# Routed experts on one core: tokens packed behind each other, gathered once, and taken by ScalarE at an address read from memory

## The chip, the cores and the metric

The kernel runs on one core of a Trainium2 chip. The metric is the device time of one execution in microseconds (us). TensorE is PE in the profile, VectorE is DVE, ScalarE is ACT, GpSimd is POOL; SyncE (SP) issues most transfers.

## The reference

Two transformer blocks over 256 tokens of width 1024, all in float32. The first mixes tokens (stick-breaking attention, an mLSTM and a spatial gate), then sends each token to 2 of 32 experts; the second has a short convolution, an attention and two convolutional feed-forward layers. Only the experts of the first block are touched here:

```python
g_top = argmax(xt @ rg_w + rg_b)                  # one of 4 groups
e_val, e_loc = top_k(e_in, 2)                     # two of its 8 experts
e_w = softmax(e_val) * g_w
hb = silu(xb @ w_gate[e]) * (xb @ w_up[e])        # xb: the tokens of expert e, 1024 -> 256
y  = y.at[row_tok].add((hb @ w_down[e]) * wt)     # 256 -> 1024, added to each token's row
```

Each expert has 3 MB of weights, 96 MB for all 32; a token goes to two of them, so an expert has 16 tokens on average.

## The kernel before, in words

**Weights.** All weights come as one stream of units of 128x2048 floats (1 MB) in the order of use. SP fetches unit n into one of four raw buffers as soon as DVE has done with unit n-4. A matmul in float32r rounds its operands, so each unit is split: ACT writes the high part (`split`, a copy with rounding, L529, or in halves at L538), DVE the low part (raw minus high, L1194, halves at L1205). High and low parts have three buffers each, freed when PE has used the unit (`unit_used`). An expert has two units for gate and up and one for down; two experts make a pair, with its six units 0 to 5: expert 0's gate-up in 0 and 1, expert 1's in 2 and 3, and the two down units in 4 and 5. There are 16 pairs. The first two and the last two are written out, the twelve between them are three rounds of a loop of four pairs on PE, ACT and DVE.

**Tokens.** The router (DVE, small operations on 128x64 and less) marks the two chosen experts of each token in `sel`. Three small matmuls (`ranked`) count the tokens of each expert ahead of each token; that count is the token's slot, and each expert has 64 slots. For a group of four experts (a quad, two pairs) `pick_quad` compares the slot numbers with 1 to 64 (L1559), which gives a 0/1 matrix of tokens by 4x64 slots. `gather` (L2431) multiplies the tokens, high part and low part, with it, one block of 128 channels at a time, into one bank of 512 columns: 256 slots of the high part and 256 of the low part. ACT (`gather_out`, L749) or DVE copies that to `xg`. A quad's eight blocks are gathered during the two pairs before it, four in each pair; so all pairs but the last two gather. Tokens above 64 for one expert go another way, behind a branch on `spill_count`; the branch is not taken with these inputs.

**A pair.** `pair_gate_up` multiplies the 64 slots, high and low as 128 columns of the array, with the high and the low part of a unit: 16 matmuls of 512 columns an expert (L2448, L2449). The result has the slots' high part in rows 0 to 63 and the low part in rows 64 to 127. ACT copies it out (`gate_up_out`, L754), PE turns its four blocks (`turn_rows`, four transposes, L2456), and DVE adds the two halves (`fold`, L1608). ACT takes SiLU of the gate half (`silu_pair`, L758), DVE multiplies with the up half (`hidden`, L1613), ACT rounds the product (`hidden_high`, L762) and DVE makes its low part (`hidden_low`, L1617). `pair_down` makes the down product, 12 matmuls an expert (L2042 to L2044). `turn_slots` turns the pick matrix, ACT copies it (`back_out`, L766), DVE sums the slots' weights (`slot_weights`). In the next pair ACT and DVE scale and split the result (`y_high`, L773, and `y_low`, L1626) and PE adds it to the tokens' rows (`scatter`, L2500, L2501).

**The order.** Every engine has its order written out by hand. In `pair_act` it is: second half of unit 0; unit 1; `y_high`; units 2 and 3; `gate_up_out` 0; unit 4; two gather evictions; SiLU 0; unit 5; `gate_up_out` 1; `hidden_high` 0; eviction; `back_out`; eviction; SiLU 1; first half of the next pair's unit 0; `hidden_high` 1. In the last two pairs unit 5 is split ahead of SiLU 0. PE does gate-up 0, scatter, two gathers, turn 0, gate-up 1, a gather, `turn_slots`, turn 1, a gather, down 0, down 1; in the last two pairs turn 0 stands between the two units of gate-up 1.

Of the kernel before, what the change touches and what calls it, by code (L numbers as in the profile page):

```python
# [119 lines left out]
ARENA = A_QKA + 8 * T  # L120
A_FINAL = 3072
# [8 lines left out]
def program(nc, stream, table, params, finals, p_in, x_in, out):  # L130
    ctx = ExitStack()
    with ctx:
# [15 lines left out]
        xres = sb("xres", [P, TT, D])  # L148
        xn = sb("xn", [P, TT, D])
# [18 lines left out]
        spill_count = sb("spill_count", [1, 1], mybir.dt.int32)  # L168
        cwn = sb("cwn", [P, 2, 12])
# [33 lines left out]
        for name, width in [("gt", 16), ("lf", 8), ("la", 8), ("ccol", 16), ("den", 8), ("ssb", 8), ("msb", 8),  # L203
# [4 lines left out]
                            ("sel", 64), ("key", 64), ("over", 64), ("spill", 1), ("wslot", 1)]:  # L208
# [54 lines left out]
        xg = [a.rearrange("p (k e w s) -> p k e w s", k=KD, e=4, w=2)  # L263
              for a in (arena_r[:, 6144:10240], xs[:].rearrange("p w k t -> p (w k t)"))]

        gu = arena[:, 0:1024].rearrange("p (e n) -> p e n", e=2)
        gut = arena[:, 1024:1536].rearrange("p (e f s) -> p e f s", e=2, f=4)
# [179 lines left out]
        def overflow_pe(pe):  # L447
            with pe.If(spilled(pe) > 0):
# [10 lines left out]
                pe.wait_ge(S("over_ready"), 1)  # L459
# [34 lines left out]
        def _(sp):  # L494
# [5 lines left out]
            sp.dma_start(cst[:, P:], table[:, P:]).then_inc(S("table_loaded"), 16)  # L500
# [15 lines left out]
        def _(act):  # L516
# [194 lines left out]
            act.dma_start(g2_row, finals[2]).then_inc(S("final_loaded"), 16)  # L711
            act.dma_start(p_t, p_in).then_inc(S("p_loaded"), 16)
# [33 lines left out]
            def gather_out(buf, k, n, at):  # L746

                act.wait_ge(S("gathered"), n)
                act.activation(xg[buf][:, k].transpose([0, 2, 1, 3]), bank[at][:].rearrange("p (w e s) -> p w e s", w=2, e=4),  # L749
                               ACT.Copy).then_inc(S("gather_out"), 1)  # L750

# [4 lines left out]
            def silu_pair(x, e):  # L756
                act.wait_ge(S("summed"), x.count(2, e + 1))
                act.activation(sgl[:, e], gut[:, e, 0:2, :], ACT.Silu).then_inc(S("pair_silu"), 1)  # L758
# [17 lines left out]
            def pair_act(x):  # L776
# [3 lines left out]
                def out(m):  # L780
                    if not x.last_quad:
                        gather_out(1 - x.buf, 4 * x.second + m, x.count(4, 9 + m), 2 + m % 2)
# [35 lines left out]
            pairs(act, pair_act)  # L818
# [256 lines left out]
        def _(pool):  # L1075
# [26 lines left out]
            ins.then_inc(S("router_scaled"), 1)  # L1102
# [81 lines left out]
        def _(dve):  # L1184
# [365 lines left out]
            dve.tensor_tensor(dv, v2, v1, ALU.subtract).then_inc(S("router_diff"), 1)  # L1550
            dve.wait_ge(S("ranked"), 1)
            dve.scalar_tensor_tensor(two(V("key")), bank[0][:, 128:192].rearrange("p (a e) -> p a e", a=TT), 1.0,
                                     sel.bitcast(F32), ALU.add, ALU.mult).then_inc(S("routed"), 1)
# [14 lines left out]
            def gather_out(k, n, at):  # L1568

                dve.wait_ge(S("gathered"), k + 1)  # L1570
                dve.tensor_copy(xg[0][:, k].transpose([0, 2, 1, 3]),
                                bank[at][:].rearrange("p (w e s) -> p w e s", w=2, e=4)).then_inc(S("gather_dve"), 1)

            dve.wait_ge(S("routed"), 2)
            pick_quad(slice(0, 4), 0, S("pick_ready"))
            token_rest(1)
            link(dve.tensor_scalar(V("over"), V("key"), float(SLOTS + 1), None, ALU.is_ge))
# [24 lines left out]
            pick_quad(slice(4, 8), 1, S("pick_ready"))  # L1602
            split_to(U_MOE + 3)

            def fold(x, e):

                dve.wait_ge(S("rows_turned"), x.count(2, e + 1))
                dve.tensor_reduce(gut[:, e], bank[e][:].rearrange("p (f w s) -> p f s w", f=4, w=2), AX.X, ALU.add)\  # L1608
                   .then_inc(S("summed"), 1)

            def hidden(x, e):
                dve.wait_ge(S("pair_silu"), x.count(2, e + 1))
                dve.tensor_tensor(hv[:, e], sgl[:, e], gut[:, e, 2:4, :], ALU.mult).then_inc(S("hidden_ready"), 1)  # L1613
# [23 lines left out]
            def pair_dve(x):  # L1637
# [10 lines left out]
                if not x.second and x.p0 and not x.last_quad:  # L1648
# [4 lines left out]
                    quad_weights(four, 1 - x.buf, S("pick_ready"))  # L1653
                ahead(2)
                ahead(3)

                if x.last_quad:
                    split_part(x.unit(4), 0)
                    fold(x, 0)
                    split_part(x.unit(4), 1)  # L1660
                    hidden(x, 0)
                    hidden_low(x, 0)
                    fold(x, 1)
                    slot_weights(x)
                    hidden(x, 1)
                    split_part(x.unit(5), 0)
                    hidden_low(x, 1)
                    split_part(x.unit(5), 1)
                    return
                fold(x, 0)  # L1670
                ahead(4)
                hidden(x, 0)
# [361 lines left out]
        def _(pe):  # L2034
# [470 lines left out]
            def pair_step(x):  # L2505
# [27 lines left out]
                if x.p0:  # L2533
                    pe.wait_ge(S("summed"), x.count(2))
# [425 lines left out]
```

## Time and profile before

| | |
|---|---|
| median of 3 runs | 1088.3 us (1086.83 to 1090.26) |
| the profiled execution | 1087.57 us, its span 1085.6 us |
| busy in the span | PE 1058.6, DVE 866.3, ACT 714.3, POOL 144.1 |
| mean granted TensorE clock | 0.996 of 2.4 GHz |
| moved from HBM | 230.85 MB |
| expert stage | from the first gate-up matmul at 156.42 us to the end of the last down product at 449.49 us, 293.1 us |

The span reaches from the first to the last instruction; what lies around it is 2.0 us. A matmul's end in the profile is modelled, so matmuls that follow each other overlap in it: the distance from start to start is what one costs. ACT's and DVE's instructions overlap a little too, by some 0.1 us.

### The profile page before, as it was taken

The numbers are of one execution on the slowest core, as the hardware profiler recorded it, in microseconds if no ns is written. First come the engines' busy times: TensorE is split into PE (matmuls) and PEld (weight loads), VectorE is DVE, ScalarE is ACT, GpSimd is POOL, SyncE is SP. The second block draws the span as 40 slices with busy tenths as digits, with TensorE's granted clock in tenths as the row PEclk, the third lists the DMA queues.
The fourth block names the chain that finished last, engine by engine and source line by source line (L and its number), as shares of the span: only waits on it lengthen the run. The fifth ranks groups of instructions, "written<-read, shape, count | busy, mean of one in ns | idle before, by whom it ended". The sixth has DMA issues, their size and how long they took to land.

```text
span 1085.6 us, 17366 instructions
## 1 busy us (share of the span) xinstructions
PE 1058.6 (98%) x6390; PEld 925.0 (85%) x6390; DVE 866.3 (80%) x1142; ACT 714.3 (66%) x962; POOL 144.1 (13%) x96
## 2 busy tenths in 40 slices
PE   7999989999999999999999999999999999999997
PEld 6877778888788887789989899998788889999986
DVE  5498689999999999877666777677777877876876
ACT  6676479898889898775435545445566766455553
POOL 3001100000000000012000334250200000432420
PEclk9999999999999999999999999999999999999999
DMA  9541528889988888754654454554433335545531
GB/s 369 189 155 39 206 82 347 348 346 333 346 331 337 343 344 334 285 209 156 225 180 178 155 213 161 206 193 155 173 137 118 116 120 211 207 156 217 184 126 40
DMA packets 33605, 232.64 MB, mean 214 GB/s; under 512 B 3856, under 2 KB 3984, under 8 KB 6032
## 3 DMA queue, kind: packets, MB, share of 16 engines
q1 hardware_dynamic: 32688, 229.98, 57.3%
q10 hardware_dynamic: 864, 1.93, 0.6%
q8 instruction: 35, 0.57, 0.2%
q14 instruction: 18, 0.15, 0.0%
HBM read 230.85 MB, written 1.05 MB: 214 GB/s over the span
## 4 chain that ended last, share of the span: by engine, by line
PE 78%; DVE 12%; ACT 5%; DMA 2%; issue 2%; POOL 0%; SPq 0%; DVEq 0%; ACTq 0%
PE bank L2042 11%; PE bank L2044 11%; PE bank L2043 11%; PE bank L2600 9%; PE bank L2601 8%; PE bank L2602 8%; DVE wlo L1194 4%; PE bank L2449 4%; PE bank L2448 4%; PE bank L2431 2%; ACT whi L529 2%; DMA raw<-stream 2%; DVE arena L1797 2%; PE bank L2456 1%; DVE wlo L1205 1%
## 5 line engine op out<-in xcount | busy, mean ns | idle before, releaser
L1194 DVE TENSOR_TENSOR wlo<-raw,whi 128x2048 fp32r<-128x2048 f32 x178 | 405.7, 2288 | 62.9 <-ACT whi L529 62.3
L529 ACT ACTIVATE whi<-raw 128x2048 fp32r<-128x2048 f32 x197 | 375.0, 1913 | 76.3 <-PE bank L2044 37.6
L2600 PE MATMUL bank<-xs,whi 128*128 128x256 f32 x896 | 251.2, 280 | 1.5 <-DVE wlo L1194 1.5
L2601 PE MATMUL bank<-xs,whi 128*128 128x256 f32 x896 | 250.2, 279 | 0.0
L2602 PE MATMUL bank<-xs,wlo 128*128 128x256 f32 x896 | 250.0, 279 | 0.0
L2600 PEld LDWEIGHTS bank<-xs,whi 128*128 128x128 f32 x896 | 168.4, 188 | 3.8 <-DVE wlo L1194 2.3
L2601 PEld LDWEIGHTS bank<-xs,whi 128*128 128x128 f32 x896 | 168.4, 188 | 0.9
L2602 PEld LDWEIGHTS bank<-xs,wlo 128*128 128x128 f32 x896 | 168.4, 188 | 0.0
L2042 PE MATMUL bank<-whi,rounded 128*128 128x512 f32 x344 | 138.4, 402 | 1.1 <-DVE wlo L1194 0.4
L2044 PE MATMUL bank<-whi,rounded 128*128 128x512 f32 x344 | 136.1, 396 | 0.0
L2043 PE MATMUL bank<-wlo,rounded 128*128 128x512 f32 x344 | 136.0, 395 | 0.0
L2042 PE MATMUL bank<-whi,xs 128*128 128x512 f32 (+1 forms) x304 | 121.0, 398 | 2.8 <-DVE xs L1312 0.9
L1155 POOL COPY cwn<-par 128x12 f32 (+1 forms) x22 | 93.3, 4247 | 199.5 <-DVE arena L1797 199.4
L2044 PE MATMUL bank<-whi,xs 128*128 128x512 f32 (+1 forms) x304 | 118.3, 389 | 0.0
L2043 PE MATMUL bank<-wlo,xs 128*128 128x512 f32 (+1 forms) x304 | 118.2, 389 | 0.0
L1797 DVE SCALAR_TENSOR_TENSOR arena<-arena,cwn 128x255 f32<-128x255 f32 (+1 forms) x160 | 66.7, 480 | 34.6 <-ACT arena L846 33.9
L846 ACT ACTIVATE arena<-arena,cwn 128x256 f32<-128x256 f32 x80 | 34.2, 499 | 86.2 <-DVE arena L1786 86.2
L1087 POOL TENSOR_SCALAR total<-sumsq 128x1 f32<-128x1 f32 x14 | 7.2, 512 | 628.7 <-ACT xn L563 628.2
L1205 DVE TENSOR_TENSOR wlo<-raw,whi 128x1024 fp32r<-128x1024 f32 x66 | 79.2, 1220 | 1.9 <-ACT whi L529 1.7
L2042 PEld LDWEIGHTS bank<-whi,rounded 128*128 128x128 f32 x344 | 64.6, 188 | 18.1 <-issue 3.6
L2044 PEld LDWEIGHTS bank<-whi,rounded 128*128 128x128 f32 x344 | 64.6, 188 | 15.6
L2043 PEld LDWEIGHTS bank<-wlo,rounded 128*128 128x128 f32 x344 | 64.7, 188 | 13.1
(342 smaller groups left out, 1655.2 us busy)
## 6 DMA issues: line engine op xcount, KB each, us to landing
raw<-stream SPq DMA_DIRECT2D x215, 1024.0 KB, 4.9
arena<-finals ACTq DMA_DIRECT2D x3, 512.0 KB, 5.6
xres<-x_in SPq DMA_DIRECT2D x2, 512.0 KB, 4.8
raw<-stream SPq DMA_DIRECT2D x4, 256.0 KB, 6.1
out<-xn SPq DMA_DIRECT2D x4, 256.0 KB, 2.1
par<-params SPq DMA_DIRECT2D x1, 844.0 KB, 12.4
cst<-table SPq DMA_DIRECT2D x1, 502.0 KB, 8.8
arena<-p_in ACTq DMA_DIRECT2D x1, 256.0 KB, 5.9
```

The source lines that it names most:

```text
L529: act.activation(whi[:, s, :], raw[:, a, :], ACT.Copy).then_inc(S("high_done"), 1)
L1155: pool.tensor_copy(cwn[:, b, :], src).then_inc(S("taps_ready"), 1)
L1194: dve.tensor_tensor(wlo[:, s, :], raw[:, unit0 % RAW, :], whi[:, s, :].bitcast(F32), ALU.subtract)\
L1205: ins = dve.tensor_tensor(wlo[:, s, w], raw[:, unit0 % RAW, w], whi[:, s, w].bitcast(F32), ALU.subtract)
L1797: ins = dve.scalar_tensor_tensor(a, fraw[:, b, f, 0:T - 2 + k], cwn[:, b, 4 * k + f:4 * k + f + 1], a, ALU.mult, ALU.add)
L2042: pe.matmul(o, ah, bh, start=start, stop=False, skip_group_check=True)
L2043: pe.matmul(o, ah, bl, start=False, stop=False, skip_group_check=True)
L2044: return pe.matmul(o, al, bh, start=False, stop=stop, skip_group_check=True)
L2448: pe.matmul(bank[e][:], tokens, whi[:, s, c], start=kk == 0, stop=False, skip_group_check=True)
L2600: pe.matmul(o, whi[:, s, w], xhi[:, kk, :], start=first, stop=False, skip_group_check=True)
L2601: pe.matmul(o, whi[:, s, w], xlo[:, kk, :], start=False, stop=False, skip_group_check=True)
L2602: ins = pe.matmul(o, wlo[:, s, w], xhi[:, kk, :], start=False, stop=kk == 7, skip_group_check=True)
```

## The change

**Places instead of slots.** All tokens of all experts are packed behind each other, expert after expert, in 512 places. DVE sums `sel`, makes a running sum over the experts (`tensor_tensor_scan`) and from it where each expert begins; two wider matmuls give each token's place (`place`) and each expert's first place (`offs`, held at most 64 below the end of what is gathered, `first_place` as integers). For a token, its two places are the largest and the rest of the sum over the experts.

**One gather.** `pick_places` makes tokens by 256 places: a mask of one place and, with it added, of the other. Half 0 (places 1 to 256) is gathered ahead of pair 0, half 1 during pairs 0 and 1, four gathers in each. Pairs 2 to 13 gather nothing. The gathered tokens lie with high and low part of one place beside each other.

**Windows.** `take(p, e)` reads the expert's first place into a register of ACT and copies the 64 places from there to `window[e]`, in two instructions of 128x512. It is done for the pair to come: expert 0's behind SiLU 1, expert 1's at the pair's end. ACT's pairs are now all written out; PE and DVE keep their loop.

**Halves summed in the turn.** `turn_rows` is four float32 matmuls with `stack`, 128x64, with a one where row // 2 equals the column: it turns and adds high and low part at once. `fold` is gone; SiLU and `hidden` read the bank.

**Order.** Turn 0 stands between the two units of gate-up 1 in every pair, SiLU 0 ahead of unit 5 in every pair, and DVE does units 4 and 5 in halves around `hidden` and `hidden_low` in every pair. The pick of a quad's slots (`pick_quad`) stays for the scatter.

```diff
-            ins.then_inc(S("routed"), 1)
+            link(ins)
+            sel_f, tot, upto_ = sel.bitcast(F32), V("tot"), V("upto_")
+            link(dve.tensor_tensor(tot, sel_f[:, 0], sel_f[:, 1], ALU.add))
+            link(dve.tensor_tensor_scan(upto_, tot, tot, 0.0, ALU.add, ALU.max))
+            dve.tensor_tensor(places[:, 0:3:2], same(upto_, NE), same(tot, NE), ALU.subtract)
+            dve.tensor_tensor(places[:, 1], upto_, sel_f[:, 1], ALU.subtract).then_inc(S("routed"), 1)
...
+            link(dve.tensor_tensor(offs, bank[0][:, 192:224], last_place, ALU.min))
+            dve.tensor_copy(first_place[:], offs[0:1, :]).then_inc(S("routed"), 1)
+            link(dve.scalar_tensor_tensor(place, bank[0][:, 128:192].rearrange("p (a e) -> p a e", a=TT), 1.0,
+                                          sel_f, ALU.add, ALU.mult))
+            dve.tensor_reduce(V("pmax"), place, AX.X, ALU.max)
+            link(dve.tensor_reduce(V("psum"), place, AX.X, ALU.add))
+            link(dve.tensor_tensor(V("pmin"), V("psum"), V("pmax"), ALU.subtract))
+
+            def pick_places(half):
+                w = slice(T * half, T * half + T)
+                for t in range(TT):
+                    ins = dve.tensor_scalar(mask[:, t], iota[:, w], V("pmax")[:, t:t + 1], None, ALU.is_equal)
+                link(ins)
+                for t in range(TT):
+                    ins = dve.scalar_tensor_tensor(gpick[half][:, t], iota[:, w], V("pmin")[:, t:t + 1], mask[:, t],
+                                                   ALU.is_equal, ALU.add)
+                ins.then_inc(S("gpick_ready"), 1)
...
+            def take(p, e):
+
+                if p == PAIRS:
+                    return
+                if p:
+                    act.wait_ge(S("unit_used"), U_MOE + 6 * (p - 1) + 2 * e + 2)
+                act.wait_ge(S("gather_out"), 6 if p < 2 else 14)
+                place = act.value_load(first_place[0:1, 2 * p + e:2 * p + e + 1], min_val=0, max_val=2 * T - SLOTS)
+                for i in range(2):
+                    act.activation(window[e][:, 4 * i:4 * i + 4, :],
+                                   xg[i].rearrange("p k s w -> p k (s w)")[:, :, bass.ds(place * 2, 2 * SLOTS)], ACT.Copy)                       .then_inc(S("window_ready"), 1)
...
-                if x.last_quad:
-
-                    ahead(5)
-                    silu_pair(x, 0)
-                else:
-                    silu_pair(x, 0)
-                    ahead(5)
+                silu_pair(x, 0)
+                ahead(5)
                 gate_up_out(x, 1)
                 hidden_high(x, 0)
                 out(2)
-                back_out(x)
                 out(3)
                 silu_pair(x, 1)
+                take(x.p0 + 1, 0)
+                back_out(x)
                 if x.p0 < PAIRS - 1:
                     round_part(x.unit(6), 0)
                 hidden_high(x, 1)
+                take(x.p0 + 1, 1)
...
-                    ins = pe.transpose(bank[e][:, P * f:P * f + P], gu[:, e, P * f:P * f + P], ident)
+                    ins = pe.matmul(bank[e][:, SLOTS * f:SLOTS * f + SLOTS], gu[:, e, P * f:P * f + P], stack, start=True,
+                                    stop=True, skip_group_check=True)
...
+                if x.p0:
+                    pe.wait_ge(S("hidden_ready"), x.count(2))
+                pair_gate_up(x, 1, (0,))
                 turn_rows(x, 0)
-                if x.p0:
-                    pe.wait_ge(S("summed"), x.count(2))
-                pair_gate_up(x, 1)
-                fetch(2)
+                pair_gate_up(x, 1, (1,))
```

## Rows read from the trace of the kernel before

**Rows 1.** The chain that ended last: start us, us, what (first down matmuls).
```profile
259.40 0.44 PE bank L2042
...
297.75 0.50 PE bank L2042
...
408.31 0.45 PE bank L2042
```

**Rows 2.** Windows, three pairs: us, PE, PEld, DVE, ACT, POOL busy, clock, DMA, GB/s.
```profile
334.60:353.00 18.40, 18.34 (x93) 15.28 (x92) 17.92 (x22) 16.54 (x21) 0.00 (x0) 1.00 0.86 335
...
413.90:431.20 17.30, 16.82 (x77) 12.97 (x76) 16.57 (x19) 14.67 (x16) 0.00 (x0) 1.00 0.86 334
431.20:449.30 18.10, 17.12 (x77) 13.00 (x76) 17.30 (x19) 12.77 (x14) 0.00 (x0) 1.00 0.94 347
```

**Rows 3.** Timeline of PE in a middle pair: start us, us, instructions [idle before].
```profile
345.83 1.13 PE L2431 MATMUL bank<-rounded,arena_r 128*128 128x256 f32 x8
346.79 0.60 PE L2456 MATMUL bank<-cst,arena 128*128 128x128 f32 x4
347.15 0.48 PE L2448 MATMUL bank<-whi,xs 128*128 128x512 f32 x1
...
350.96 0.64 PE L2431 MATMUL bank<-rounded,arena_r 128*128 128x256 f32 x4
```

**Rows 4.** Timeline of ACT in the same pair.
```profile
345.80 1.92 ACT L529 ACTIVATE whi<-raw 128x2048 fp32r<-128x2048 f32 x1
347.61 1.09 ACT L749 ACTIVATE arena_r<-bank 128x512 fp32r<-128x512 f32 x2
349.14 0.31 ACT L758 ACTIVATE arena<-arena 128x128 f32<-128x128 f32 x1 [0.45 <-DVE arena L1608]
```

**Rows 5.** Timeline of ACT and PE in pair 14, and behind pair 15.
```profile
424.16 0.58 ACT L754 ACTIVATE arena<-bank 128x512 f32<-128x512 f32 x1
...
424.79 0.66 PE L2456 MATMUL bank<-cst,arena 128*128 128x128 f32 x4 [0.35 <-ACT arena L754]
...
426.21 0.31 ACT L758 ACTIVATE arena<-arena 128x128 f32<-128x128 f32 x1 [0.77 <-DVE arena L1608]
...
426.43 1.05 ACT L538 ACTIVATE whi<-raw 128x1024 fp32r<-128x1024 f32 x1
...
427.38 0.29 ACT L762 ACTIVATE rounded<-arena 128x128 fp32r<-128x128 f32 x1
...
427.58 1.05 ACT L538 ACTIVATE whi<-raw 128x1024 fp32r<-128x1024 f32 x1
...
452.92 1.09 ACT L826 ACTIVATE arena<-bank 128x512 f32<-128x512 f32 x2 [0.33 <-PE bank L2044]
```

**Rows 6.** Timeline of DVE in a middle pair.
```profile
341.95 1.41 DVE L1626 SCALAR_TENSOR_TENSOR rounded<-bank,sm,rounded 128x512 fp32r<-128x512 f32 x2
343.27 0.75 DVE L1559 TENSOR_TENSOR rounded<-cst,sm 128x256 fp32r<-128x256 f32 x2
...
344.02 4.49 DVE L1194 TENSOR_TENSOR wlo<-raw,whi 128x2048 fp32r<-128x2048 f32 x2
348.43 0.68 DVE L1608 TENSOR_REDUCE arena<-bank 128x256 f32<-128x512 f32 x1
```

**Rows 7.** Timeline from the router's last steps to the end of pair 0.
```profile
148.86 0.23 DVE L1552 SCALAR_TENSOR_TENSOR sm<-bank,rounded 128x64 f32<-128x64 f32 x1 [0.38 <-PE bank L2420]
149.12 0.76 DVE L1559 TENSOR_TENSOR rounded<-cst,sm 128x256 fp32r<-128x256 f32 x2
...
156.42 0.39 PE L2448 MATMUL bank<-whi,arena_r 128*128 128x512 f32 x1
...
173.37 1.27 ACT L773 ACTIVATE rounded<-bank,sm 128x512 fp32r<-128x512 f32 x2 [0.82 <-PE bank L2044]
```

**Rows 8.** Waits from 200 to 430 us: us in total, times, longest.
```profile
ACT whi L529 <- DMA raw<-stream: 3.2, 5, 1.2
```

More of the change, by code:

```diff
@@ L780, in out @@
                 def out(m):
[L781 to L782 removed]
+                    if x.p0 < 2:
+                        gather_out(1, 4 * x.second + m, x.count(4, 9 + m), 2 + m % 2)
                 if x.p0:
@@ L817, in _ @@
             act.activation(V("m")[:, 0:1], Q("g0")[:, 0:1], ACT.Silu)
-            pairs(act, pair_act)
+            act.wait_ge(S("gather_dve"), 2)
+            act.wait_ge(S("routed"), 2)
+            take(0, 1)
+            for p0 in range(PAIRS):
+                pair_act(Pair(p0))
             assert done[0] == U_PLEP
@@ L1570, in gather_out @@
                 dve.wait_ge(S("gathered"), k + 1)
[L1571 to L1575, printed above, removed]
+                dve.tensor_copy(xg[k // 4][:, k % 4, 0:T, :].transpose([0, 2, 1]),
+                                bank[at][:].rearrange("p (w s) -> p w s", w=2)).then_inc(S("gather_dve"), 1)
+            pick_places(0)
             token_rest(1)
+            link(dve.tensor_tensor(cand, same(offs, NE), sel_f, ALU.mult))
+            dve.tensor_tensor(two(V("key")), place, cand, ALU.subtract).then_inc(S("routed"), 1)
+            dve.wait_ge(S("routed"), 3)
             link(dve.tensor_scalar(V("over"), V("key"), float(SLOTS + 1), None, ALU.is_ge))
@@ L2431, in gather @@
                         ins = pe.matmul(bank[at][:, T * h:T * h + T], src[:, t, w],
-                                        pick[:, buf, t].rearrange("p e s -> p (e s)"), start=h == 0 and t == 0,
+                                        gpick[half][:, t], start=h == 0 and t == 0,
                                         stop=h == 1 and t == 1, skip_group_check=True)
@@ L2445, in pair_gate_up @@
                         kk = 4 * i + k
-                        tokens = xg[x.buf][:, kk, 2 * x.second + e].rearrange("p w s -> p (w s)")
+                        tokens = window[e][:, kk, :]
+                        if x.p0 == 0 and e == 0:
+                            tokens = xg[i][:, k, 0:SLOTS].rearrange("p s w -> p (s w)")
                         c = slice(512 * k, 512 * k + 512)
@@ L2475, in pair_down @@
                 pe.wait_ge(S("turned_ready"), x.count(2, e + 1))
-                halved = e == 1
-                s = x.unit(5)[0] % RING if halved else wait_unit(x.unit(4 + e))
+                s = x.unit(4 + e)[0] % RING
                 w = slice(SLOTS * e, SLOTS * e + P)
-                for c, f in [(c, f) for f in range(2) for c in range(2)] if halved else \
-                        [(c, f) for c in range(2) for f in range(2)]:
-                    if e == 0 and f == 0 and not x.last_quad:
+                for c, f in [(c, f) for f in range(2) for c in range(2)]:
+                    if e == 0 and f == 0 and x.p0 < 2:
                         pe.wait_ge(S("gather_out"), x.count(4, 9 + c))
-                    if halved and (c, f) == (0, 1):
-                        wait_unit(x.unit(5))
+                    if (c, f) == (0, 1):
+                        wait_unit(x.unit(4 + e))
                     v = slice(D * f + 512 * c, D * f + 512 * c + 512)
```

135 lines of the change are left out of this document (66 added, 69 removed).

## The prediction

> **What bounds the kernel now.** Only the expert stage changes, so I read it from the outside in. The chain that ended last gives the pace: the first matmul of a pair's down product starts at 297.75 and at 408.31, six pairs apart, so a pair takes 18.43 us; the two pairs from 259.40 to 297.75 took 38.35, 1.5 more [rows 1]. The windows say who is full: in a pair of 18.40, PE was busy 18.34, DVE 17.92, ACT 16.54, DMA 0.86. In the last two pairs, which have no gather, it was 16.82 of 17.30 and 17.12 of 18.10 [rows 2]. So PE sets the pace of the fourteen gathering pairs, with DVE and ACT close behind, and once the gather is gone PE is no longer the bound: something else holds a pair at 17.3 to 18.1. The reader should see that margin first: the most that the last pairs' form shows is 1.1 us a pair, not the whole of PE's saving.
>
> **What the change takes away.** PE: pairs 2 to 13 lose four gathers of four matmuls. Eight of these take 0.96 (345.83 to 346.79) [rows 3], so 1.92 a pair. DVE: two folds a pair. The fold stands between the row turn and the SiLU and held back a SiLU by 0.45 to 0.77 [rows 4, 5]; its 0.68 less the 0.08 by which DVE's instructions overlap is 0.60 [rows 6], so 1.2 of DVE's 17.9. ACT: four gather evictions a pair, two of them in 1.09, so about 0.5 each, 2.0 [rows 4].
>
> **What it adds to ACT.** Four window copies a pair, each 128x512 from SBUF to SBUF. Such a copy of 1024 columns takes 1.05 and of 128 columns 0.30 [rows 5], by a straight line 0.62 for 512, 0.5 from start to start. That is 2.0, so ACT's sum does not fall at all; the copies only move. And two register loads a pair, 31 in all. No row times one. Below: the kernel makes one such load and a branch on ACT ahead of the eviction at 452.92, and that started 0.03 after the matmul it waits for, so zero can be. Above: ACT was idle 0.33 there [rows 5], so at most about 0.33. A register in an address costs nothing by itself: DVE's picks at a loop's register took 0.75 for two, at a fixed address 0.76 [rows 6, 7]. I take zero for the load, as each stands behind a copy or SiLU that waits anyway, and keep 31 x 0.33 = 10.2 us for the range.
> The Trainium skill (Runtime: NRT & Kernel Launch, Instruction fetch mechanics) gives about 200 ns for a register load from HBM; by that, if nothing hid it, the sum would be 6.2 us higher, an estimate. No row here shows such a load.
>
> **What it moves, and why that decides.** The turn of expert 0's rows goes from before the second expert's gate-up (346.79, ahead of the matmul at 347.15 [rows 3]) to behind its first unit. But ACT has that SiLU ahead of its split of unit 5, whereas in the last two pairs of before the split went first. So ACT must now stand still until PE has done unit 2, and that closes a ring through three engines, once a pair. From one SiLU of expert 0 to the next:
> ACT: SiLU 0.2, split of unit 5 1.81 (345.80 to 347.61) [rows 4], eviction of expert 1 until its rows are turned and SiLU can start 1.32 (424.16 to 424.79, 0.66 for the four turns, 0.03) [rows 5], SiLU 0.2, window copies for expert 0 1.0, eviction of the turned slots 0.3, first half of the next unit 0.95, rounding of the hidden rows 0.2 (426.43 to 427.38 to 427.58 [rows 5] gives both), window copies for expert 1 1.0, second half 0.95, split of unit 1 1.92. Sum 9.85.
> DVE: 0.03, low part of unit 1 2.2, two y_low 1.32, in every second pair the picks 0.75, low part of unit 2 2.29 [rows 6]. Sum 5.84, or 6.59.
> PE: 0.14 and 0.08 to start, eight matmuls at 3.81 / 16 = 0.238, so 1.9, four turns 0.60 [rows 3], 0.03. Sum 2.75.
> Together 18.44, and 19.19 with picks: 18.8 in the mean, against 18.43. DVE reaches unit 1 by another way at nearly the same time (from the hidden rows' rounding: its low part, a half of unit 5, slot weights, two halves of the next unit, 4.1 against ACT's 4.1), so shortening ACT a little would not help. The folds' removal is already counted in this, and PE's 1.92 is spent waiting for unit 2. Pairs 2 to 13: 12 x 0.4 = +4.7.
>
> **The other terms.** Router: ahead of the rank matmuls DVE adds a sum, a scan and two subtractions, each at the small operations' 0.26 from start to start (148.86 to 149.12), about +0.85. Behind them, in place of one operation before the pick: offsets, place, two reductions, a subtraction (1.2), then two masks and two picks of 128x256 at the pick's 0.76 for two, 1.6 in all where 0.76 was [rows 7]. So +0.85 + 1.0 + 0.8 = +2.6, on the path, since PE can only fill meanwhile. Pair 0: ACT does a window copy pair (1.0) before its first split, DVE the second half's picks (1.5) and a quad pick before it gets to the hidden rows; PE's unit 2 then ends near 166.8 (first gate-up at 156.42 + 2.6; DVE's unit 1, picks and unit 2 follow one another), and from the SiLU at 167.4 the same ring with gathers is 10.5 to the pair's end, 177.9, where before it was 173.4 [rows 7]: +4.5 with the +2.6 inside. Pair 1 has gathers and copies both: two evictions (1.0) and 0.5 of gathers in the ring, +1.8. Pair 14: 18.4 against 17.3, +1.1. Pair 15 makes no copies: 0. The late constants are one more transfer on ACT's queue long before they are read: 0.
> Small unknowns: the turn is now an fp32 product of 64 columns. Below, the turn's 0.09 each; above, 0.24, that of a 512-column matmul [rows 3]; it stands in the ring twice, so 0 to +1.2 a pair; I take 0, a transpose of twice the width being nearest. The first gathers' evictions write every second word: 0.5 to 1.0 each, 0.5 taken. The hidden product reads PSUM: 0.3. ACT no longer loops: 0 to -1.5 us, if the 1.5 lost once in [rows 1] was ACT's jump; DVE and PE keep theirs, so 0.
> On that the Trainium skill (same page and section) says that a taken branch to a page not held forces a fetch and straight code is prefetched; by that rule the sum would be up to 1.5 lower. The trace shows one long pair of pairs, not whose jump.
>
> **Sum.** 4.5 + 1.8 + 4.7 + 1.1 = +12.1 on the profiled execution's 1087.57: 1099.7, say 1100. That execution is 0.7 below the median of 1088.3, which stays inside this measure.
>
> **The rivals.**
> A, the forecast: the ring through ACT, DVE and PE, 1094 to 1107 (18.4 to 19.3 a pair).
> B, ends on the other side: the ring is not closed, because ACT reaches the SiLU late enough or DVE early enough that PE's saving comes through. Then a pair goes like the last two of before, less the folds, plus picks: 17.6. 12 x (17.6 - 18.43) = -10, front and first pairs +5: 1082. It decides if the ring is shorter than 18.0. For it: the last pairs' 17.3 [rows 2]. Against it: these had ACT's split of unit 5 ahead of the SiLU and no copies, 2.0 less on an ACT that is in the ring. If PE alone were the bound it would be 12 x -1.92 = -23, 1070; DVE's 16.7 a pair speaks against it.
> C, register loads in the open: two a pair, both in the ring, 0.33 each: 1110, and more with slower turns, 1107 to 1125.
> D, nearly nothing: 18.1 a pair, -4 against the front's +5 and the first pairs: 1085 to 1093.
> E, HBM: at 0.86 to 0.94 DMA share [rows 2] and 3.2 us of ACT's waits for raw units in 230 us [rows 8] there is room for 18, little for 17; it caps B near 17.2 and changes nothing in A.
>
> **How the numbers follow.** A 0.48, C 0.17, D 0.17, B 0.18 (E within B). About 0.3% (3.3 us) is what a measurement of this kernel tells from no change: faster is below 1085.0, slower above 1091.6. B gives 0.18 and the edge of D 0.02 to faster, 0.20; the rest of D nearly all to same, 0.13; A and C and the upper edge of D to slower, 0.67. The range leaves half of B below and half of C above: 1083 to 1114. A alone, 1094 to 1107.
>
> **What would show it.** Between two pairs' first down matmuls 18.4 and 19.2 in turn; ACT idle about 2 us before each expert-0 SiLU, released by the row turn; PE idle before units 0, 1 and 2, released by DVE's low parts; window copies of 0.6; the first gate-up 2.6 later. It would be wrong if ACT's idle before that SiLU is under 0.5 (ring open, B), if it has gaps before the copies with no releaser (C), or if the four turns take over 0.9.

## The result, and the profile after

The changed kernel takes 1124.81 us in the median (1124.07 to 1125.4, 4 runs), the kernel before 1087.57 (1085.91 to 1090.26, 4 runs) on the same chip: ratio 1.0346, 95% interval 1.0333 to 1.036. So it is 37 us slower. I had said 1100 with a range to 1114: the direction holds, the size does not. The profiled execution took 1125.4, its span 1123.5, at a clock of 0.996.

All of the loss is in the expert stage. ScalarE's timeline marks the end of each pair by `y_high` (L803, before L773): pairs 0, 1, 13, 14 and 15.

```profile
179.70 1.25 ACT L803 ACTIVATE rounded<-bank,sm 128x512 fp32r<-128x512 f32 x2
...
202.12 1.25 ACT L803 ACTIVATE rounded<-bank,sm 128x512 fp32r<-128x512 f32 x2
...
448.12 1.24 ACT L803 ACTIVATE rounded<-bank,sm 128x512 fp32r<-128x512 f32 x2
...
468.24 1.24 ACT L803 ACTIVATE rounded<-bank,sm 128x512 fp32r<-128x512 f32 x2
...
487.06 1.27 ACT L803 ACTIVATE rounded<-bank,sm 128x512 fp32r<-128x512 f32 x2 [2.84 <-PE bank L2084]
```

Before, the same five stood at 173.37 [rows 7], 191.67, 414.15, 431.44 and 449.52. The stage ends 37.54 later: 6.33 by pair 0, 4.12 in pair 1, 23.52 in pairs 2 to 13 (20.50 each where it was 18.54), 2.83 in pair 14, 0.74 in pair 15. Behind the stage the two kernels run alike: 636.4 and 636.1 us to the span's end.

The windows of two middle pairs, to lay beside [rows 2]:

```profile
355.20:375.30 20.10, 17.69 (x80) 13.29 (x80) 16.96 (x20) 16.58 (x20) 0.00 (x0) 1.00 0.78 294
375.30:395.40 20.10, 18.09 (x86) 14.03 (x86) 16.21 (x17) 16.65 (x20) 0.00 (x0) 1.00 0.82 315
```

Nobody is full any more: the busiest engine has 2 us idle in 20.1, and the DMA share is at 0.8. A ring of waits would look like this: each engine stands still once a round for another (e1 to e5 and e11 test it below). The clock is 1.00, so it isn't that. The table of waits (200 to 430 us) names the ring's members:

```profile
ACT arena L788 <- PE bank L2503: 35.8, 22, 2.8
DVE rounded L1669 <- ACT rounded L792: 28.6, 22, 1.8
...
PEld bank L2494 <- DVE wlo L1236: 13.7, 12, 1.1
...
PEld bank L2494 <- DVE wlo L1225: 10.6, 17, 0.9
...
ACT xn_r L779 <- issue: 4.9, 11, 0.7
```

SiLU waits for TensorE's row turn (35.8 us in 11 pairs, 3.3 a pair, both experts together), the gate-up matmuls for VectorE's low parts, VectorE for ScalarE. The last row is of another kind: "issue" is a wait without a releaser. ScalarE's timeline over one pair shows its place:

```profile
335.06 0.28 ACT L788 ACTIVATE arena<-bank 128x128 f32<-128x128 f32 x1 [2.66 <-PE bank L2503]
335.24 1.91 ACT L546 ACTIVATE whi<-raw 128x2048 fp32r<-128x2048 f32 x1
337.04 0.59 ACT L784 ACTIVATE arena<-bank 128x512 f32<-128x512 f32 x1
337.52 0.31 ACT L792 ACTIVATE rounded<-arena 128x128 fp32r<-128x128 f32 x1
338.82 0.28 ACT L788 ACTIVATE arena<-bank 128x128 f32<-128x128 f32 x1 [1.00 <-PE bank L2503]
339.52 0.64 ACT L779 ACTIVATE xn_r<-arena_r 128x512 fp32r x1 [0.42 <-issue]
340.07 0.62 ACT L779 ACTIVATE xn_r<-xs 128x512 fp32r x1
340.59 0.37 ACT L796 ACTIVATE rounded<-bank 128x256 fp32r<-128x256 f32 x1
...
344.00 1.90 ACT L546 ACTIVATE whi<-raw 128x2048 fp32r<-128x2048 f32 x1
...
355.18 0.28 ACT L788 ACTIVATE arena<-bank 128x128 f32<-128x128 f32 x1 [2.04 <-PE bank L2503]
```

From SiLU 0 to SiLU 0 it is 20.12; the reader can walk my ring down this list. SiLU 1 to the first window copy takes 0.70, where the SiLU that a split follows takes 0.18 (335.06 to 335.24). What fills the gap is the register load (view of line L777, ScalarE's sequencer, 22 loads from 200 to 430 us; minimum, median, maximum in ns):

```profile
L777 ACTq TENSOR_LOAD <-first_place x22: 272/273/286, 216.0 to 421.6; - x22
L777 ACTq FUSED_REGOPS  x22: 152/152/152, 216.3 to 421.9; - x22
```

In this pair the load started at 338.9, behind the start of SiLU 1 at 338.82. So its 0.27 and the 0.15 of address arithmetic were not done in the 1.00 us in which ScalarE waited for SiLU 1: they came after it. `take` has a wait of its own ahead of the load, for the pair's unit 1, but TensorE had ended that unit some 9 us before. This is the sign that the prediction named for rival C, gaps before the copies with no releaser. The load for expert 1 costs nothing, since it stands behind copies and splits that are still at work. TensorE's timeline in the same pair, the turns of expert 1 and of expert 0, and the instruction behind the latter:

```profile
337.68 1.10 PE L2503 MATMUL bank<-arena 128*128 128x64 f32 x8 [0.40 <-ACT arena L784]
...
354.14 1.00 PE L2503 MATMUL bank<-arena 128*128 128x64 f32 x8
```

The code has four matmuls there; the trace has eight. The next one starts 0.81 later (at 354.95) where four transposes took 0.36 [rows 3], and SiLU 0 starts 1.04 behind the turn's start where the forecast had 0.63. Even so the columns are half as many as a transpose's. Per record it is nearly the same, 0.81 / 8 = 0.10 against 0.36 / 4 = 0.09; there are twice as many records.

### The profile page after: what moved, and what is told of

It is laid out like the page before. It is cut to its first block, busy times and chain, and to the rows that moved or that the text cites. A ratio compares the mean times of both kernels' runs of the same rounds, so it can differ in the third digit from the quotient of the medians.

```text
span 1123.5 us, 17298 instructions
## 1 busy us (share of the span) xinstructions
PE 1063.7 (95%) x6330; PEld 914.2 (81%) x6330; DVE 853.6 (76%) x1143; ACT 721.6 (64%) x976; POOL 144.7 (13%) x96
## 3 DMA queue, kind: packets, MB, share of 16 engines
HBM read 231.16 MB, written 1.05 MB: 207 GB/s over the span
## 4 chain that ended last, share of the span: by engine, by line
PE 66%; DVE 18%; ACT 8%; issue 5%; ACTq 1%; DMA 1%; POOL 0%; DVEq 0%; SPq 0%
PE bank L2082 9%; PE bank L2084 9%; PE bank L2083 9%; PE bank L2640 8%; PE bank L2641 8%; PE bank L2642 8%; DVE wlo L1225 6%; DVE wlo L1236 4%; ACT whi L546 3%; PE bank L2494 3%; PE bank L2503 3%; PE bank L2495 2%; DVE arena L1837 2%; ACTq L777 1%; ACT whi L555 1%
## 5 line engine op out<-in xcount | busy, mean ns | idle before, releaser
L1225 DVE TENSOR_TENSOR wlo<-raw,whi 128x2048 fp32r<-128x2048 f32 x164 | 373.5, 2287 | 57.5 <-ACT whi L546 57.1
L2494 PE MATMUL bank<-whi,xn_r 128*128 128x512 f32 x248 | 102.9, 415 | 15.1 <-DVE wlo L1236 10.9
L1236 DVE TENSOR_TENSOR wlo<-raw,whi 128x1024 fp32r<-128x1024 f32 x94 | 113.4, 1220 | 0.4
L2495 PE MATMUL bank<-wlo,xn_r 128*128 128x512 f32 x248 | 98.1, 395 | 0.0
L2082 PEld LDWEIGHTS bank<-whi,rounded 128*128 128x128 f32 x344 | 64.7, 188 | 33.9 <-DVE rounded L1669 19.5
```

Source lines behind the costliest of these rows:

```text
L1225: dve.tensor_tensor(wlo[:, s, :], raw[:, unit0 % RAW, :], whi[:, s, :].bitcast(F32), ALU.subtract)\
L1236: ins = dve.tensor_tensor(wlo[:, s, w], raw[:, unit0 % RAW, w], whi[:, s, w].bitcast(F32), ALU.subtract)
L2082: pe.matmul(o, ah, bh, start=start, stop=False, skip_group_check=True)
L2494: pe.matmul(bank[e][:], tokens, whi[:, s, c], start=kk == 0, stop=False, skip_group_check=True)
L2495: ins = pe.matmul(bank[e][:], tokens, wlo[:, s, c], start=False, stop=kk == 7, skip_group_check=True)
```

## The experiments

The pace is the mean from SiLU 0 of pair 2 to that of pair 13, over 11 pairs, in the profiled execution. Before: 18.52, or 18.39 without 1.5 us of late weights (see "Small terms" below). After: 20.43. The kernel before ran beside each batch, with medians of 1087.02 (e1 to e4), 1087.21 (e5 to e8) and 1086.40 (e9 to e12). The ratios are to these; "less" below is the difference to the changed kernel's 1124.81.

| run | median us | ratio to before (95%) | pace |
|---|---|---|---|
| e1 row turn as transposes | 1112.75 | 1.0235 (1.0198 to 1.0273) | 19.57 |
| e2 no register load | 1117.16 | 1.0276 (1.0238 to 1.0314) | 19.88 |
| e3 no copies, no loads | 1101.69 | 1.0134 (1.0099 to 1.0169) | 18.82 |
| e4 e1 and e3 | 1094.66 | 1.0068 (1.0045 to 1.0091) | 18.40 |
| e5 turn 0 before unit 2 | 1121.06 | 1.0315 (1.0296 to 1.0333) | 20.05 |
| e6 loads early | 1117.12 | 1.0276 (1.0257 to 1.0295) | 19.87 |
| e7 copies on GpSimd | 1106.35 | 1.0176 (1.0158 to 1.0193) | 19.10 |
| e8 e5, e7, VectorE's order | 1090.11 | 1.0029 (1.0018 to 1.0041) | 18.16 |
| e9 before, no gathers | 1084.88 | 0.9991 (0.9975 to 1.0007) | 18.16 |
| e10 before, halves summed in the turn | 1096.19 | 1.0091 (1.0073 to 1.0109) | 19.07 |
| e11 copies in ScalarE's waits | 1104.69 | 1.0172 (1.0154 to 1.0191) | 18.82 |
| e12 e11, e5, VectorE's order | 1090.99 | 1.0049 (1.0024 to 1.0073) | 18.21 |

**e1: the row turn as four transposes.** SiLU and the hidden product read the first 64 of each block's 128 turned rows, with no sum of the halves, so the experts' result is of half of the window's places (not of the high parts, as the expectation has it: high and low part of a place lie side by side).

```diff
-                    ins = pe.matmul(bank[e][:, SLOTS * f:SLOTS * f + SLOTS], gu[:, e, P * f:P * f + P], stack, start=True,
-                                    stop=True, skip_group_check=True)
+                    ins = pe.transpose(bank[e][:, P * f:P * f + P], gu[:, e, P * f:P * f + P], ident)
```

> The changed kernel with the row turn made by four transposes again, as before the change; SiLU and the hidden product read the slots' high half alone, so the low half's share of each product is left out. Everything else stays. Theory R (a ring of waits, once a pair: expert 0's SiLU on ScalarE, its split of unit 5, SiLU 1, window copies, split of unit 1, VectorE's low parts of units 1 and 2, TensorE's unit 2 and the turn, SiLU 0 again): the turn stands twice in the ring, and as a float32 product it shows eight pieces where a transpose shows four, so 0.44 us each more. The pace falls from 20.45 us by 0.8 to 0.9 a pair, the kernel by 11 to 14 us, to about 1112. Rival T (the turn is TensorE's own load and TensorE is not the bound; it hides in its idle time): under 3 us.

12.1 us less, and 0.86 off the pace, as the ring theory has it; rival T (under 3 us) is out. ScalarE from a SiLU 0 at 347.05 on:

```profile
347.22 1.91 ACT L546 ACTIVATE whi<-raw 128x2048 fp32r<-128x2048 f32 x1
349.03 0.58 ACT L784 ACTIVATE arena<-bank 128x512 f32<-128x512 f32 x1
349.50 0.31 ACT L792 ACTIVATE rounded<-arena 128x128 fp32r<-128x128 f32 x1
350.36 0.28 ACT L788 ACTIVATE arena<-bank 128x128 f32<-128x128 f32 x1 [0.55 <-PE bank L2503]
351.06 0.64 ACT L779 ACTIVATE xn_r<-arena_r 128x512 fp32r x1 [0.43 <-issue]
```

Eviction to SiLU 1 is 1.33, the 1.32 of the forecast; with the fp32 turn it is 1.78. The load's gap stays.

**e2: windows at a fixed place.** The copies are made, at an address that the code holds (place 14 m for expert m), so of other places.

```diff
-                place = act.value_load(first_place[0:1, 2 * p + e:2 * p + e + 1], min_val=0, max_val=2 * T - SLOTS)
+                place = 14 * (2 * p + e)
```

> The changed kernel with each window taken at a fixed place (14 times the expert's number) in place of the address read from memory: 31 register loads gone, the tokens are not the right ones, all copies stay. Theory R: ScalarE's idle 0.42 us before the first copy of each pair goes, 0.5 a pair in the ring, so 6 to 9 us for the kernel, to about 1117. Rival H (the loads are hidden behind waits of ScalarE): under 2 us.

7.7 us less, 0.55 off the pace: one load a pair, not two, is in the ring, at about 0.5. Rival H (under 2 us) is out.

**e3: no window copies and no loads from pair 2 on** (those pairs use old windows).

```diff
-                if p == PAIRS:
+                if p == PAIRS or p > 1:
```

> The changed kernel with the window copies and their register loads left out from pair 2 on: TensorE multiplies the same old windows. Theory R: 2.0 of copies and 0.5 of load leave the ring, but VectorE's way round (low part of expert 1's hidden rows, second half of unit 5, two halves of the next unit 0) is nearly as long, so the pace falls by 1.4 to 1.8 a pair only, the kernel by 20 to 26 us, to about 1102. Rival P (the pace is TensorE's or the transfers'): under 8 us.

23.1 us less, 1.61 off the pace. ScalarE lost 2.1 + 0.5 of ring work and the ring only 1.6: the rest is VectorE's own way to unit 1, which the prediction had as nearly as long. In this run VectorE works without a pause from the low part of expert 0's hidden rows (344.13) to unit 1 (350.80) and beyond.

**e4: e1 and e3 together.**

> Both of the last: no window copies from pair 2 on and the turn by transposes with the low half left out. Theory R: the kernel falls by 28 to 33 us, to about 1094, so even with neither copies nor long turns the pace stays at 18 us or more, because the ring still runs through VectorE's order; TensorE's saving of 1.9 a pair does not come. Rival S (copies and turns are all that is wrong): pace 17 or less, 45 us or more, to 1080.

30.2 us less, inside the 28 to 33; rival S (45 or more) is out. Of what is left over the kernel before, 7.6 us, none is in the middle pairs' pace (18.40). By the end of pair 1 the run is 6.7 behind (`y_high` at 198.41 and 191.67): it is the front and the first two pairs.

**e5: turn 0 ahead of unit 2.**

```diff
-                pair_gate_up(x, 1, (0,))
                 turn_rows(x, 0)
+                pair_gate_up(x, 1, (0,))
```

> The changed kernel with expert 0's row turn ahead of the second expert's gate-up again, as before the change, instead of behind its first unit. Nothing is left out. Theory R: the ring no longer passes VectorE's low part of unit 2 and TensorE's unit 2, but the way from ScalarE's copies through VectorE's halves to the down product is nearly as long, and the turn waits for the eviction: the pairs with picks gain 0.6, the others 0.1, about 5 us in all, to 1120. Rival O (the place of the turn is all that closes the ring): 12 x 1.5, 15 to 25 us, to 1105.

3.8 us less only, though it takes 1.9 us of matmuls out of the way between low part and SiLU 0. The idle ahead of SiLU 0 falls from 2.0 to 2.8 down to 0.3 and less, but the wait has only moved to the next instruction:

```profile
350.31 0.28 ACT L788 ACTIVATE arena<-bank 128x128 f32<-128x128 f32 x1 [0.23 <-PE bank L2503]
352.30 1.92 ACT L546 ACTIVATE whi<-raw 128x2048 fp32r<-128x2048 f32 x1 [1.71 <-PE bank L2495]
```

The split of unit 5 writes into the high-part buffer of unit 2 (there are three), and that is free only when TensorE has used unit 2. From 200 to 430 us this costs ScalarE 17.8 us in 11 pairs. So the ring still passes through TensorE's unit 2; the place of the turn was not all that closed it, and rival O is out.

**e6: the loads early.** Both loads of a pair stand ahead of the last steps where ScalarE is still busy; the copies take the kept registers.

```diff
-                place = act.value_load(first_place[0:1, 2 * p + e:2 * p + e + 1], min_val=0, max_val=2 * T - SLOTS)
+                place = at[e]
```

> The changed kernel with both register loads of a pair moved to ScalarE's stream behind the splits of units 2 and 3, where work is queued ahead of them; the copies stay where they are. Nothing is left out. Theory R and the run without loads: the loads hide behind 1.9 us splits, so the 0.5 a pair goes as it did at fixed addresses: 1116 to 1118. Rival Q (a register load holds ScalarE's queue wherever it stands): two loads in the open, 0 to 5 us slower than the changed kernel, 1125 to 1130.

The same 7.7 us as e2, with the computation whole. So the load costs nothing to be seen where the engine has work in its queue, and 0.5 a pair behind an instruction that waits. Rival Q (a load holds the queue wherever it stands) is out.

**e7: the window copies on GpSimd**, with GpSimd's own register loads.

```diff
+                for i in range(2):
+                    pool.tensor_copy(window[e][:, 4 * i:4 * i + 4, :],
+                                     xg[i].rearrange("p k s w -> p k (s w)")[:, :, bass.ds(place * 2, 2 * SLOTS)])\
+                        .then_inc(S("window_ready"), 1)
```

> The changed kernel with window copies and register loads on GpSimd, which has no work in this stage; each starts as soon as TensorE has used the window. Nothing is left out. GpSimd's 128x384 copies took 0.57 each in the trace of before, so 0.75 for 512, four in a pair 3.0 of 18. Theory R: as the run without copies (1101.7), and 2 to 3 us less for pairs 0 and 1, which had copies there: 1097 to 1101. Rival G (GpSimd's copies take far longer, or slow VectorE's instructions down while they run): low parts of 2.29 get longer, 1105 to 1125.

5 us over the upper end of the main expectation, inside the rival's. Against e3 the pace is 0.28 a pair longer, 3.4 us in 12 pairs, and the 2 to 3 us expected from pairs 0 and 1 did not come (`y_high` of pair 1 at 199.88, in e3 at 199.64). GpSimd's timeline, then VectorE's rows at the same time:

```profile
358.53 2.50 POOL L1164 CAST xn_r<-arena_r 128x512 fp32r x1 [11.39 <-PE bank L2502]
360.99 2.67 POOL L1164 CAST xn_r<-xs 128x512 fp32r x1
365.68 0.61 POOL L1164 CAST xn_r<-arena_r 128x512 fp32r x1 [2.03 <-PE bank L2502]
366.24 0.61 POOL L1164 CAST xn_r<-xs 128x512 fp32r x1
```

```profile
353.89 2.29 DVE L1232 TENSOR_TENSOR wlo<-raw,whi 128x2048 fp32r<-128x2048 f32 x1
...
358.27 4.91 DVE L1232 TENSOR_TENSOR wlo<-raw,whi 128x2048 fp32r<-128x2048 f32 x2
...
366.68 0.31 DVE L1676 TENSOR_TENSOR rounded<-arena,rounded 128x128 fp32r<-128x128 f32 x1 [1.33 <-ACT rounded L792]
```

The same copy takes 0.61 when VectorE is idle (it was from 365.35 to 366.68) and 2.5 to 2.67 beside VectorE's subtraction; and two of these take 4.91 where they took 4.49 [rows 6].

**e8: e7, e5, and VectorE splits the first half of the down units ahead of its hidden product.**

```diff
-                hidden(x, 0)
                 split_part(x.unit(4), 0)
-                hidden_low(x, 0)
+                hidden(x, 0)
                 split_part(x.unit(4), 1)
-                hidden(x, 1)
+                hidden_low(x, 0)
                 split_part(x.unit(5), 0)
-                hidden_low(x, 1)
+                hidden(x, 1)
                 split_part(x.unit(5), 1)
+                hidden_low(x, 1)
```

> The run with GpSimd's copies, with VectorE's first half of each down unit ahead of the hidden product that waits for SiLU (instead of behind it) and the turn of expert 0 ahead of the second gate-up. Nothing is left out. Theory R: VectorE's idle of 1.2, 1.1 and 1.5 us a pair goes, the pace falls to 17.7 to 17.9: 1083 to 1089, so no more than the kernel before, since the turns' 1.7 us a pair on TensorE take back what the gathers gave. Rival B (the order was all that kept the gather's 1.9 from coming through): 1065 to 1075.

1090.11: 34.7 us under the changed kernel, 1 us over the upper end of what I expected, and still 3 over the kernel before. Two pairs' windows:

```profile
351.20:369.59 18.39, 17.77 (x86) 13.98 (x85) 18.14 (x18) 14.61 (x18) 6.67 (x5) 1.00 0.93 348
369.59:387.41 17.82, 17.47 (x86) 14.14 (x85) 17.44 (x21) 14.50 (x17) 5.99 (x5) 1.00 0.90 348
```

In the pair with picks VectorE, slowed by GpSimd, is full; in the other TensorE and VectorE both have under 0.4 us left. So rival B (1065 to 1075) is out.

**e9: the kernel before without its gathers from pair 2 on** (their matmuls and evictions are left out; those pairs use old tokens).

```diff
-                fetch(0)
-                fetch(1)
+                if x.p0 < 2:
+                    fetch(0)
+                    fetch(1)
```

> This is the kernel before with the gathers and their evictions left out from pair 2 on (those pairs compute with tokens gathered earlier, so the output is of the wrong tokens). It measures what the packing could have bought at all. Theory 1, VectorE and the ring bound the kernel before nearly as tightly as TensorE does (a pair of 18.3 us shows VectorE 17.9 busy): the gathers' matmuls, about 1.9 us a pair, come back only as 1.5 to 3 us in all, 1084.5 to 1086. Theory 2, TensorE alone is the bound: most of 12 x 1.9 us comes through, 1065 to 1070.

This is what "gathered once" could buy in the old order, at no cost for windows, places or picks, and it is 1.5 us, with an interval that holds no change. (The execution profiled took 1082.95, the fastest of ten, so its pace of 18.16 flatters it.) A pair's window:

```profile
323.00:341.00 18.00, 16.74 (x78) 13.19 (x77) 17.60 (x22) 14.51 (x17) 0.00 (x0) 1.00 0.90 347
```

TensorE fell from 18.34 to 16.74 and the pair from 18.4 to 18.0: VectorE's 17.60 was right behind. The theory that TensorE alone was the bound (1065 to 1070) is gone. VectorE isn't quite full either; from 200 to 430 us ScalarE's SiLUs waited 30.6 us for VectorE's `fold`, 25 times, so its place in VectorE's order counts too. How much each holds is not shown.

**e10: the kernel before with the halves summed in the turn**, and `fold` gone.

```diff
-                    ins = pe.transpose(bank[e][:, P * f:P * f + P], gu[:, e, P * f:P * f + P], ident)
+                    ins = pe.matmul(bank[e][:, SLOTS * f:SLOTS * f + SLOTS], gu[:, e, P * f:P * f + P], C("stack"), start=True,
+                                    stop=True, skip_group_check=True)
```

> This is the kernel before with one part of the change alone: the two halves of the hidden product are summed in the rows' turn, in TensorE, and VectorE's add of them goes. Theory 1: each fp32 turn takes about 0.45 us more than four transposes did, so about 0.9 us a pair comes onto TensorE, which is the engine with least room; 12 to 14 pairs make +10 to +14 us, about 1098 to 1101. Rival: the add that goes shortens VectorE's way between the two turns by more than the turns grow, and the kernel gets faster, about 1080.

9.8 us slower than the kernel before, just under the 10 to 14 of the sum; the rival (faster) is out.

```profile
339.22:358.30 19.08, 19.08 (x102) 16.12 (x102) 16.82 (x20) 16.44 (x21) 0.00 (x0) 1.00 0.85 323
```

TensorE is busy 19.08 of 19.08 and VectorE, with 1.1 less to do, waits. This part of the change costs by itself, in the old order 9.8 us; in the new one going back to transposes, with the sum left out, gave 12.1 (e1).

**e11: loads early, and the copies in ScalarE's own waits**: expert 0's ahead of SiLU 0, expert 1's ahead of SiLU 1 (the windows of pair 2, copied in pair 1, keep their place).

```diff
+                if x.p0 != 1:
+                    take(x.p0 + 1, 0)
                 silu_pair(x, 0)
```

> The changed kernel with the register loads done early and the window copies moved into waits that ScalarE has anyway: expert 0's ahead of the pair's first SiLU (2.0 to 2.7 us of idle time there), expert 1's ahead of the second SiLU (1.0 us idle). Ring theory: per pair the exposed load (0.4 to 0.5 us) and about 1.1 us of copies leave the ring, 1.5 x 14 = 21 us, about 1103 to 1105. Rival, ScalarE's total work counts and not its place in the ring: 1116 to 1118, as with the loads early alone.

1104.69, as the ring says; its pace is that of e3, 18.82, with all copies made. The rival is out: not ScalarE's sum of work counted, but where in the ring it stood. Against e6, which has the loads early too (19.87), the place of the copies alone is worth 1.05 a pair.

**e12: e11 with e5 and VectorE's order.** The edits are those of e8 and e11.

> The same, and also the two rearrangements that were tried with the copies on GpSimd: VectorE splits the first half of the down unit ahead of its hidden product, and the first turn is issued ahead of the last gate-up matmuls of its unit. With GpSimd out of VectorE's way the pace should be that of the earlier such run (18.1 us a pair, 1090) or a little under: ScalarE's own copies lie in idle time. 1087 to 1091. Rival: the slowing of VectorE by GpSimd was all that held that run up, and this one ends clearly under the kernel before, about 1080. Other rival: the copies ahead of the SiLUs delay them, 1095 to 1100.

1090.99, inside the 1087 to 1091. Without GpSimd beside it VectorE has room again, but the run isn't under e8. Windows of a plain pair and of the pair behind it that was not plain:

```profile
280.63:298.40 17.77, 17.42 (x86) 14.11 (x85) 16.72 (x19) 16.52 (x22) 0.00 (x0) 1.00 0.94 361
298.40:318.74 20.34, 18.98 (x86) 15.23 (x84) 16.41 (x21) 16.52 (x21) 0.00 (x0) 0.92 0.85 301
```

At 17.8 a pair TensorE is again at 17.4 of it. And the weights now come late at times; ScalarE's and TensorE's timelines, then one-microsecond windows (the clock is the third column from the right):

```profile
299.87 1.91 ACT L546 ACTIVATE whi<-raw 128x2048 fp32r<-128x2048 f32 x1 [1.19 <-DMA raw<-stream]
```

```profile
302.31 1.10 PE L2518 MATMUL bank<-arena 128*128 128x64 f32 x8 [1.36 <-ACT arena L790]
303.23 0.70 PE L2097 MATMUL bank<-whi,rounded 128*128 128x512 f32 x1
303.73 0.63 PE L2098 MATMUL bank<-wlo,rounded 128*128 128x512 f32 x1
```

```profile
301.00:302.00 1.00, 0.00 (x0) 0.00 (x0) 0.00 (x0) 1.00 (x2) 0.00 (x0) 1.00 1.03 410
...
304.00:305.00 1.00, 1.00 (x3) 0.72 (x3) 1.00 (x2) 1.00 (x3) 0.00 (x0) 0.50 1.03 426
305.00:306.00 1.00, 1.00 (x4) 0.80 (x3) 0.95 (x5) 1.00 (x2) 0.00 (x0) 0.50 0.58 246
```

A unit 1.2 us late left TensorE idle 1.36, and behind that it ran at 0.50, its 1.2 GHz level, from about 303.3 to 306.7. This pair and the next took 4.1 us more than two of 17.8. In an execution without it the kernel would be near 1089 (an estimate: 1092.71, the profiled one, less 4.1), and the fastest of the six took 1089.51: still 2 to 3 us above the kernel before.

## Why the prediction was right and wrong

**What bounds before: right.** "PE is no longer the bound: something else holds a pair at 17.3 to 18.1" is what e9 shows, 18.0 without any gather. Rival B's basis (the order of the last pairs) and D's 18.1 were sound readings; what they left out was the ring and its costs. B as a whole did not come: the ring was closed.

**The ring: right in kind.** Its three engines, its closing wait (SiLU 0 for the turn behind unit 2) and its steps are in the rows above. With the two mis-sized terms out, the pace is 20.43 - 0.86 (e1) - 0.55 (e2) = 19.0, worked out, against the 18.8 of the forecast. Of its signs, ScalarE's 2.0 to 2.8 us of idle time ahead of each SiLU 0, released by the row turn, came true. The alternation of 18.4 and 19.2 is there too, at 20.1 and 20.8.

**Turns: the step that failed first.** "I take 0, a transpose of twice the width being nearest." It is 0.46 and 0.41 in the ring, 0.87 a pair; the bound of 1.2 held it. The nearest row was another, and it was in the trace of before: the router's matmuls, plain float32, 36 columns.

```profile
139.56 0.98 PE L2400 MATMUL bank<-rw,arena 128*128 128x36 f32 x8
140.37 0.63 PE L2387 MATMUL bank<-cst,xres 128*128 128x128 f32 x4
```

The code has four matmuls here, the trace eight, and the next begins 0.81 later, exactly what a row turn takes now. I took the likeness in shape; the likeness that counted was the kind of product.

**Register loads: the step that failed second.** "No row times one" is false. The view of `spill_count` in the trace of before has one on ScalarE:

```profile
L361 ACTq TENSOR_LOAD <-spill_count x1: 490/490/490, 449.6 to 449.6; - x1
```

It lay at 449.6, while ScalarE was at work on `y_high` (449.52 to 450.79), and left no idle of its own: hence my zero, from the eviction behind it. And zero because "each stands behind a copy or SiLU that waits anyway" has it the wrong way round: behind a SiLU that waits, the load waits too. Measured: 0.52 for the one in the open (0.70 less 0.18), nothing for the other, 0.55 of pace and 7.7 us in all. My bound was 0.33 for each. The Trainium skill (Runtime: NRT & Kernel Launch, Instruction fetch mechanics) gives about 200 ns for a register load from HBM. This one, of a value in SBUF, took 273, with 152 of arithmetic behind it, and it was the place that decided.

**Small terms.** Window copies 0.62 long, 0.52 from start to start: as forecast. VectorE's way to unit 1 was 0.17 longer than ScalarE's, which I had as equal: its low part began at 346.11, 0.21 behind the end of ScalarE's split, and where VectorE waits for a split it starts 0.04 behind it. First gate-up at 160.03 against 156.42: 3.6 where I had 2.6; but the router's first step was already 1.04 late (144.68 to 143.64), in code that the change doesn't touch, so the edit's own 2.57 is right. It is whole at 11.85 us already: the first 512-column matmul starts 0.29 later than before (10.05 to 9.76), with the first constants, and the four behind it take 1.80 from start to start where they took 1.01. In other runs with the edit (e2, e3, e5, e7) the same step stood at 143.87 to 143.96, so most of it is of that execution and not of the edit.

And the 1.5 us that [rows 1] lost once was no jump of ScalarE's. In that stretch of the trace of before ScalarE waited four times for weights, 2.4 us in all; the longest:

```profile
288.27 1.92 ACT L529 ACTIVATE whi<-raw 128x2048 fp32r<-128x2048 f32 x1 [1.23 <-DMA raw<-stream]
```

So the 0 to -1.5 that I kept for the end of ScalarE's loop had no basis in that row.

**Sum.** Forecast and measured: pair 0 with the front 4.5 and 6.3, pair 1 1.8 and 4.1, pairs 2 to 13 4.7 and 23.5, pair 14 1.1 and 2.8, pair 15 0 and 0.7. Of the 18.8 missed in pairs 2 to 13, turns are 10.3 (12 x 0.86), loads 6.6 (12 x 0.55), and the 0.17 of VectorE's way 2.0. Pair 0's 6.3 holds the late start's 1.0. Rival C had the right sign for a price in the open, and its upper end of 1125 is where the time lies; I gave it 0.17 and let the range cut it at 1114. In truth A and C hold together, and the chances should have let both unknown terms be large at once.

**Where the expected gain went.** Off the path, by e9: 1.9 us a pair of TensorE's time was worth 0.4 at most (18.52 to 18.16; 0.2 against the 18.39 without late weights). Of that time 0.9 is given back in the two turns (twice 0.81 less 0.36; e10 shows 0.74 more busy), so that even the best order (e12, 17.8 a pair) has TensorE at 17.4; and the front and the first two pairs cost 6.7 us in e4 and 8.8 in e12 (`y_high` of pair 1 at 200.49). No version here that computes the whole result beats the kernel before. Not tried: letting TensorE read the packed tokens at an address from a register, without copies; and e12 with transposes and a fold, which e10 speaks for; but VectorE, at 16.72 of 17.77 in e12, would be full with the folds' 1.2 (an estimate), so a gain is not shown.

## To carry to other kernels

Before taking work off the fullest engine, ask how full the second is: with VectorE at 17.6 of 18.0 the first engine's 1.9 us bought at most 0.4. When an order makes a ring through three engines, put new work where an engine already waits: the same four copies cost 1.05 us a pair behind SiLU 1 (e6), 1.6 with a load in the open, and nothing to be seen ahead of the SiLUs (e11 has the pace of e3, which has no copies). An engine that no longer waits in one place may wait at the next, as for a buffer in e5. For an operation that a trace seems not to have, look for it by kind (plain float32 product, register load), not by shape, and in the sequencers' rows too.

## What the runs showed of the hardware that I had not expected

- A plain float32 matmul is two records in the trace. Four of 64 columns take 0.81, as do four of 36; four transposes of 128 columns, one record each, take 0.36. So a record is 0.10 with 36 and with 64 columns, and a transpose's with 128 is 0.09.
- A register load (0.27) with its arithmetic (0.15) on ScalarE did not begin before a waiting ACTIVATE ahead of it had begun: 0.42 idle behind SiLU 1 (e2 and e6 each won 7.7 us).
- GpSimd and VectorE slow each other: GpSimd's copy of 128x512 from 0.61 to 2.67, VectorE's two subtractions from 4.49 to 4.91 (e7). Which resource they share, no run here shows.
- After 1.36 us of idle time in a stage that was otherwise full, TensorE's granted clock fell to 0.50 for 3.4 us (e12). In the changed kernel's middle pairs none of its waits was over 1.1 us, and the clock stayed at 1.00; it did so too behind a wait of 1.26 in pair 1 (until 198.80).
